# Index scores of a sparse-attention layer: the first two of eight heads weighted and added by GpSimd, one pair of tiles ahead

## What is computed

```python
s_idx = jnp.einsum('bqhd,bld->bqhl', qi, k_idx)            # 8 heads of 64
score = jnp.einsum('bqh,bqhl->bql', wi.astype(jnp.float32),
                   jax.nn.relu(s_idx).astype(jnp.float32))
score = jnp.where(causal[None], score, -jnp.inf)
_, sel = lax.top_k(score, k_top)
```

## Time and profile before

| | |
|---|---|
| median of 3 runs | 4091.65 us (4081.93, 4091.65, 4094.02) |
| the profiled execution | 4080.8 us, its span 4078.9 us |
| busy, share of the span | TensorE 86%, VectorE 52%, ScalarE 50%, GpSimd 12% |
| score stage, first matmul to last causal addition | 366.5 to 534.7 us, 168.2 us (4.1% of the span) |

### The profile page before, as it was taken

One profiled execution on the slowest core, in us unless ns is written; L12 is line 12 of the kernel. 1 busy time (PEld: TensorE's weight loads), 2 busy tenths in 40 slices (PEclk: granted clock), 3 DMA queues, 4 the chain that ended last, 5 costly groups with the idle time before them and its releaser, 6 DMA issues. The chain is left out here.

```text
span 4078.9 us, 63641 instructions
## 1 busy us (share of the span) xinstructions
PE 3498.6 (86%) x18242; PEld 2550.7 (63%) x18242; DVE 2130.1 (52%) x5809; ACT 2029.8 (50%) x3495; POOL 500.9 (12%) x544
## 2 busy tenths in 40 slices
PE   5385979887599999999695899999978888889699
PEld 5274645446466666666584688889945555555587
DVE  0434979999555555555464100000057777777344
ACT  0433868993477777777324111111146666666222
...
GB/s 116 183 92 171 31 194 226 228 164 188 73 83 83 80 80 82 79 79 63 170 169 123 65 72 72 72 75 68 62 64 45 46 50 45 45 45 28 134 144 103
DMA packets 395849, 406.94 MB, mean 100 GB/s; under 512 B 73200, under 2 KB 317328, under 8 KB 394128
## 3 DMA queue, kind: packets, MB, share of 16 engines
...
## 5 line engine op out<-in xcount | busy, mean ns | idle before, releaser
L1013 DVE CUSTOM_DVE_ANT_0 a_att_sb_lg<-a_att_ps_s,mask 128x512 f32<-128x512 f32 (+3 forms) x512 | 302.2, 595 | 234.7 <-PE a_att_ps_s L907 193.8
L505 ACT ACTIVATE b_qkgv_sb_o_lo<-b_qkgv_ps_acc 128x512 f32<-128x512 f32 x128 | 76.7, 599 | 636.8 <-PE b_qkgv_ps_acc L488 471.7
L1044 DVE MEMSET b_att_sb_mx<- 128x256 f32 x1 | 0.3, 272 | 721.0 <-PEq L88 721.0
L1087 ACT ACTIVATE a_att_sb_pT<-a_att_ps_t 128x512 f32<-128x512 f32 (+3 forms) x640 | 315.0, 530 | 105.0 <-PE a_att_ps_t L923 98.5
L1079 ACT ACTIVATE b_att_sb_lg<-b_att_sb_lg,b_att_sb_negm 128x384 f32<-128x384 f32 (+15 forms) x256 | 305.7, 1199 | 107.6 <-DVE b_att_sb_negm L1021 106.8
L1015 DVE TENSOR_SCALAR_CACHE_REDUCE b_att_sb_lg<-b_att_ps_s 128x512 f32<-128x512 f32 (+3 forms) x512 | 289.8, 591 | 132.3 <-PE b_att_ps_s L912 128.3
L1079 ACT ACTIVATE a_att_sb_lg<-a_att_sb_lg,a_att_sb_negm 128x384 f32<-128x384 f32 (+15 forms) x256 | 307.4, 1201 | 79.5 <-DVE a_att_sb_negm L1021 79.5
L923 PE MATMUL a_att_ps_t<-ident,a_att_sb_lg 128*128 128x128 f32 x2176 | 339.8, 279 | 0.0
L906 PE MATMUL a_att_ps_s<-a_att_sb_k,a_att_sb_q 128*128 128x512 f32 (+3 forms) x640 | 287.1, 449 | 61.3 <-DMA a_att_sb_k<-scratch_kT 41.7
L912 PE MATMUL b_att_ps_s<-b_att_sb_k,b_att_sb_q 64*128 64x512 f32 (+3 forms) x1280 | 319.7, 585 | 15.3 <-DMA b_att_sb_k<-scratch_kT 9.8
L1434 DVE TENSOR_SCALAR_CACHE_REDUCE mask<-scores,threshold_bits 128x384 bf16<-128x384 f32 (+8 forms) x288 | 322.6, 1186 | 1.2
...
## 6 DMA issues: line engine op xcount, KB each, us to landing
...
a_att_sb_q<-scratch_qT SPq DMA_DIRECT2D x128, 128.0 KB
a_att_sb_q<-scratch_qT SPq DMA_DIRECT2D x256, 64.0 KB
...
```

The source lines that it names most:

```text
L1013: x = nc.vector.tensor_tensor_reduce(out, src, tab, 1.0, 2 * NEG, ALU.add, ALU.max, top[:, col:col + 1])
L1087: nc.scalar.activation(pT[:, r % 2, a:z, c:c + P], t_ps[:, n % TR, 0:z - a], ACT.Copy).then_inc(t_left, 1)
```

## The change

The heads of every tile are divided: heads 0 and 1 go to GpSimd, heads 2 to 7 stay with VectorE. GpSimd weights head 0 straight into the tile's scores (L1178 of the changed kernel), weights head 1 in place in a ring of its own, `pool_relu` (L1180), and adds it to the scores (L1184). That is 14 + 14 TENSOR_SCALARs and 14 TENSOR_TENSORs. VectorE's separate first head (L1199) is gone; its first addition of a tile, head 2, waits for GpSimd's addition of head 1. ScalarE writes each relu to the ring of the engine that will take it.

`units` has a new order. The 28 GpSimd units of all pairs and the 84 VectorE units are two lists; the first four GpSimd units (pair 0) come first, and then one GpSimd unit stands behind the first of every three VectorE units, so that GpSimd's units of a pair lie among VectorE's units of the pair before. The load of a tile's queries now waits for `until[i - 4]`, the last unit of the tile whose buffer it takes.

```diff
--- before.py
+++ after.py
@@ -1128,14 +1128,25 @@
     with Stage(nc, sems, "score") as st:
         k_hh, k_ll = (st.sb(n, [P, T], F32R) for n in ("k_hh", "k_ll"))
         q = st.sb("q", [P, 4, IH, P], F32R)
-        relu = st.sb("relu", [P, 2, T], F32)
+        relu, pool_relu = st.sb("relu", [P, 2, T], F32), st.sb("pool_relu", [P, 2, T], F32)
         causal = st.sb("causal", [P, P], F32)
         s_ps = st.ps("s", [P, 2, 4 * 512])
-        k_in, scored, relued, summed, hidden, causal_step = (
-            st.sem(n) for n in ("k_in", "scored", "relued", "summed", "hidden", "causal_step"))
+        k_in, scored, relued, summed, pooled, pool_step, hidden, causal_step = (
+            st.sem(n) for n in ("k_in", "scored", "relued", "summed", "pooled", "pool_step", "hidden", "causal_step"))
         q_in = [st.sem(f"q_in{u}") for u in range(4)]
 
-        units = [(i + e, SELECTING[i + e], h) for i in range(0, len(SELECTING), 2) for h in range(IH) for e in range(2)]
+        BY_POOL = 2
+        pool_units = [(i + e, SELECTING[i + e], h) for i in range(0, len(SELECTING), 2) for h in range(BY_POOL) for e in range(2)]
+        dve_units = [(i + e, SELECTING[i + e], h) for i in range(0, len(SELECTING), 2) for h in range(BY_POOL, IH) for e in range(2)]
+        EACH = len(dve_units) // len(pool_units)
+
+        units = pool_units[:2 * BY_POOL]
+        for x, unit in enumerate(dve_units):
+            units.append(unit)
+            if x % EACH == 0 and 2 * BY_POOL + x // EACH < len(pool_units):
+                units.append(pool_units[2 * BY_POOL + x // EACH])
+        place = {unit: n for n, unit in enumerate(units)}
+        until = [1 + max(n for n, (i, _, _) in enumerate(units) if i == tile) for tile in range(len(SELECTING))]
         block = st.block()
 
         @block.sync
@@ -1146,7 +1157,7 @@
                 sp.dma_start(k_ll[rows].bitcast(F32), kidxT[1]).then_inc(k_in, 16)
             for i, b in enumerate(SELECTING):
                 if i >= 4:
-                    sp.wait_ge(scored, 2 * IH * (i // 2 - 1))
+                    sp.wait_ge(scored, until[i - 4])
                 for part in range(2):
                     sp.dma_start(q[part * ID:(part + 1) * ID, i % 4].bitcast(F32),
                                  qidx[part].rearrange("(h d) t -> d h t", d=ID)[:, :, b * P:(b + 1) * P]).then_inc(q_in[i % 4], 16)
@@ -1158,6 +1169,19 @@
 
             nc.gpsimd.affine_select(out=causal[:], in_=causal[:], compare_op=ALU.is_ge, fill=LOWEST, base=0,
                                     pattern=[[-1, P]], channel_multiplier=1).then_inc(causal_step, 1)
+            steps = 0
+            for x, (i, b, h) in enumerate(pool_units):
+                w, N = widx[:, b, h:h + 1], (b + 1) * P
+                out = scores[:, mask_offset(b):mask_offset(b) + N]
+                pool.wait_ge(relued, place[i, b, h] + 1)
+                if h == 0:
+                    nc.gpsimd.tensor_scalar(out, pool_relu[:, x % 2, 0:N], w, None, ALU.mult).then_inc(pooled, 1)
+                else:
+                    nc.gpsimd.tensor_scalar(pool_relu[:, x % 2, 0:N], pool_relu[:, x % 2, 0:N], w, None, ALU.mult).then_inc(pool_step, 1)
+                    steps += 1
+                    pool.wait_ge(pool_step, steps)
+                    pool.wait_ge(pooled, x - 1)
+                    nc.gpsimd.tensor_tensor(out, out, pool_relu[:, x % 2, 0:N], ALU.add).then_inc(pooled, 1)
 
         @block.tensor
         def _(pe):
@@ -1177,32 +1201,38 @@
         def _(act):
             for n, (i, b, h) in enumerate(units):
                 act.wait_ge(scored, n + 1)
-                if n >= 2:
-                    act.wait_ge(summed, n - 1)
-                nc.scalar.activation(relu[:, n % 2, 0:(b + 1) * P], s_ps[:, n % 2, 0:(b + 1) * P], ACT.Relu).then_inc(relued, 1)
+                if h < BY_POOL:
+                    x, out = pool_units.index((i, b, h)), pool_relu
+                    if x >= 2:
+                        act.wait_ge(pooled, x - 1)
+                else:
+                    x, out = dve_units.index((i, b, h)), relu
+                    if x >= 2:
+                        act.wait_ge(summed, x - 1)
+                nc.scalar.activation(out[:, x % 2, 0:(b + 1) * P], s_ps[:, n % 2, 0:(b + 1) * P], ACT.Relu).then_inc(relued, 1)
 
         @block.vector
         def _(dve):
-            def hide_later_keys(n):
-
-                _, b, _ = units[n]
+            def hide_later_keys(x):
+
+                _, b, _ = dve_units[x]
                 z = mask_offset(b) + (b + 1) * P
-                dve.wait_ge(summed, n + 1)
+                dve.wait_ge(summed, x + 1)
                 nc.vector.tensor_tensor(scores[:, z - P:z], scores[:, z - P:z], causal[:], ALU.add).then_inc(hidden, 1)
 
             dve.wait_ge(causal_step, 2)
-            for n, (i, b, h) in enumerate(units):
+            for x, (i, b, h) in enumerate(dve_units):
                 w, N = widx[:, b, h:h + 1], (b + 1) * P
                 out = scores[:, mask_offset(b):mask_offset(b) + N]
-                dve.wait_ge(relued, n + 1)
-                if h == 0:
-                    nc.vector.tensor_scalar(out, relu[:, n % 2, 0:N], w, 0.0, ALU.mult, ALU.add).then_inc(summed, 1)
+                dve.wait_ge(relued, place[i, b, h] + 1)
+                if h == BY_POOL:
+                    dve.wait_ge(pooled, pool_units.index((i, b, BY_POOL - 1)) + 1)
                 else:
-                    dve.wait_ge(summed, n - 1)
-                    nc.vector.scalar_tensor_tensor(out, relu[:, n % 2, 0:N], w, out, ALU.mult, ALU.add).then_inc(summed, 1)
-                if n and units[n - 1][2] == IH - 1:
-                    hide_later_keys(n - 1)
-            hide_later_keys(len(units) - 1)
+                    dve.wait_ge(summed, x - 1)
+                nc.vector.scalar_tensor_tensor(out, relu[:, x % 2, 0:N], w, out, ALU.mult, ALU.add).then_inc(summed, 1)
+                if x and dve_units[x - 1][2] == IH - 1:
+                    hide_later_keys(x - 1)
+            hide_later_keys(len(dve_units) - 1)
             dve.wait_ge(hidden, len(SELECTING))
 
 
```

## The result

| | before | after |
|---|---|---|
| median time | 4089.24 us (4081.93 to 4094.02, 5 runs) | 4167.19 us (4159.79 to 4171.69, 5 runs) |
| score stage, first matmul to last causal addition | 168.0 us | 228.1 us |
| from there to the second attention | 2450.8 us | 2451.3 us |
| second attention, first matmul to last | 798.3 us | 817.5 us |
| behind it, to the end of the span | 295.2 us | 300.6 us |

A forecast was written before the change was run, and what follows sets the result against it. VectorE sets the score stage's pace; sharing turns with GpSimd, both engines' work sums: 197.6 - 6.5 + 4 + 1 = 196.1 us against 168.2, 27.9 us more. On a 4091.65 us median: 4120 us, range 4101 to 4156.

The forecast's parts named there:

- VectorE keeps 124.7 us: Score stage: VectorE sheds 14 first weightings and 14 of 98 additions, together 32.0 us, and keeps 124.7 us.
- The additions at 39.3 us: Score stage: GpSimd's 14 additions, priced by its TENSOR_TENSOR rows, take 39.3 us.
- The weightings at 33.6 us: Score stage: GpSimd's 28 weightings, priced like a CAST, take 33.6 us; at the two-input price 78.7 us.
- Handovers, -6.5: Score stage: turns between VectorE and GpSimd begin slightly before the other's end, taking 6.5 us off the sum.
- Idle, +4: Score stage: time in which neither VectorE nor GpSimd has work adds 4 us, ends 0 and 13.1.
- Query loads, +1: Score stage: query loads moved closer to their use make TensorE late at first, adding 1 us, ends 0 and 6.
- ScalarE and TensorE covered: Score stage: ScalarE's 131.8 us of relus lie beside a sum of 196; TensorE's lower clock costs at most a few us.
- Nothing behind the stage changes ... so this goes into the time one to one: After the score stage: a barrier closes it, so the 27.9 us more pass unchanged into the whole time.
- rival C: Score stage: VectorE and GpSimd run side by side after all; stage 148 to 152 us, time 4072 to 4076; chance 0.02.
- Rival A: Score stage: GpSimd's weighting costs more than a CAST, up to 45.1 us more, 4165 us; chance 0.14.
- B: Score stage: only two-input additions exclude each other; time 4087 to 4100 us, no difference; chance 0.07.
- D: Whole change: it doesn't do what it says, against 42 instructions on GpSimd and 28 fewer on VectorE; no chance kept.

The follow-up runs named there:

- e2_empty: The changed kernel with all 42 GpSimd instructions one column wide, heads 0 and 1 left out of the scores; 4119.52 us, ratio 1.0079, stage 179.6 us.
- f3_copy: The changed kernel with GpSimd's 28 weightings replaced by plain copies of the same shape; 4139.80 us, ratio 1.0124, stage 200.4 us.
- e6_queries: The changed kernel with six query buffers instead of four; 4164.11 us, ratio 1.019, stage 226.2 us.
- e7_empty_queries: e2_empty with six query buffers instead of four; 4104.49 us, ratio 1.0045, stage 164.3 us.
- f2_order: The kernel before with the change's unit order and query-load release, all eight heads on VectorE; 4107.16 us, ratio 1.0044, stage 185.7 us.
- g3_change_pad43: The full change with 43 memsets of 128x1 added on VectorE at the score stage's start; 4153.07 us, ratio 1.0145, stage 228.9 us.
- g1_pad43: e7_empty_queries with 43 memsets of 128x1 added on VectorE at the score stage's start; 4087.90 us, ratio 0.9992.

## Why the prediction was wrong

The direction and the mechanism held: the two engines take turns at the port, VectorE's relief is worth nothing, and the sum of both engines' work sets the stage. Point by point:

1. **VectorE keeps 124.7 us**: right. It is busy for 124.65 us in e2_empty, where nothing stands in its way.
2. **The additions at 39.3 us**: right in size (42.7 with standing), and held to 0.20 us before the end.
3. **The weightings at 33.6 us: this step failed.** A weighting is not a CAST. It costs 2.5 ns a column and 0.28 us, an estimated 93 us for the 28 where nothing is in the way. That is above even the end that I took for the largest, 78.7, the two-input price: the nearest row did not bound an operation that the trace didn't have. The error was smaller in the stage than on GpSimd, because the port is free in part of a weighting: 58.5 us of hold. Whole durations would have given 124.7 + 39.3 + 93 = 257 us, the holds give 222.5, measured are 228.1; f3_copy puts the term's share of the miss at 27.7 us.
The Trainium skill ("GPSIMD Engine Reference", section "Performance versus the Vector engine") has 1.03 cycles a column for loops of at most two operations and a best case of some 1.8. By the first, the weighting would have been the CAST's equal; measured it is 2.5 ns, at the page's 1.2 GHz an estimated 3.0 cycles. The page's price is not what this instruction has, with a number per query or a constant.
4. **Handovers, -6.5**: the additions of the change and the copies of f3_copy let VectorE in 0.13 to 0.21 us before their end, which the term had right, but a weighting lets it in 0.4 to 1.9 us early. (The 0.17 us of the prediction is a small misreading: GpSimd's second multiplication ended at 1020.40 us, not 1020.45, which makes it 0.22 and the term about a microsecond larger.)
The Trainium skill ("SBUF — State Buffer", section "Who interferes with whom") has the lock held for the whole instruction. The additions come near to that, the weightings do not, as the rows at 400.50 and 402.30 us show.
5. **Idle, +4**: too small. VectorE's first addition starts 8.5 us after the first matmul, since it waits for GpSimd's first tile; GpSimd holds the port for an estimated 2 of them, by the holds above, so some 6 us of the start are time in which nobody holds it. The order of the rows had shown this wait; it had no term. In f3_copy all the rest, this included, came to 4.3 us over the sum.
6. **Query loads, +1**: right here (1.9 us by e6_queries), and right for the reason given, that others wait anyway. With free ports they cost 15.3 us (e7_empty_queries against e2_empty) or 17.7 (f2_order); rival C's 12 us were near that.
7. **ScalarE and TensorE covered**: right, though the granted clock of the stage went from 0.98 to 0.86.
8. **"Nothing behind the stage changes ... so this goes into the time one to one": this step failed too**, and with it the same sentence ahead of the prediction. Barriers keep work apart, not the place of the code. 43 instructions fewer on VectorE moved its code loads through the second attention, which cost 14 us (g3_change_pad43 against the change, 4153.07 and 4167.19) of the 78.

Added up: 28 us that the sum had, 4 of its other terms, 28 of the weighting and 14 of the code's place make 74 of 78; the rest is within the scatter of the runs. **Rival A** was the nearest, with the right cause. That its 4165 us is 2 from the result is luck: its price was too low for GpSimd and too high for the port, and it had nothing for the second attention. With 0.14 it had too little chance: an operation without a row of its own deserved more. B is true of the last part of each weighting only, and too little of it; D fell with the counts. C's 4072 to 4076 us was out of reach in this order of the units even without contention: e7_empty_queries, with next to no work on GpSimd and no late loads, has a stage of 164.3 us where C had 148 to 152, and g1_pad43 gives for it the time of the kernel before.
